# TensorE makes the level products of a head two at a time, at four places of its slabs instead of seven

## The chip, the cores and the metric

One core of one Trainium2 chip runs the whole program. The metric is the device time of that core in microseconds (us), the median of the runs. Every time below that is not a run's time is read from one profiled execution.

## The reference

One decoder layer over 1024 tokens of width 2048: an RMSNorm, one input projection whose columns feed two groups of heads (8 HGRN2 heads with a 128x128 state, 4 GLA heads with a 128x256 state), a gated linear recurrence per head, a per-head RMSNorm times SiLU(gate), the output projection, and a gated embedding on top. What the level products belong to is this part:

```python
b = jnp.cumsum(g_c, axis=2)                       # running sum of the log decay
diff = b[:, :, :, None, :] - b[:, :, None, :, :]
decay = jnp.where(causal, jnp.exp(jnp.where(causal, diff, 0.0)), 0.0)
attn = jnp.einsum('bhik,bhjk,bhijk->bhij', q_c, k_c, decay)
o = (jnp.einsum('bhij,bhjv->bhiv', attn, v_c)
     + jnp.einsum('bhik,bhkv->bhiv', q_c * jnp.exp(b), S))
```

## The kernel before

**Tiling.** The tokens are done in two halves of 512, `h` = 0 and 1. All large projections are made of slabs: a slab is 128 output columns times 2048 input rows, and TensorE makes it in 16 steps of `k`, each of three full-width matmuls (low weights with high activations, high with low, high with high; L505 to L507), so 48 matmuls of 512 columns into `acc[par]`. An HGRN head of the input projection takes 4 slabs, a GLA head 6.

**The recurrence rides on the slabs.** While TensorE makes the slabs of head `r0`, the recurrence of the head before it, `R = r0 - 1`, is done. Its TensorE work is hung on slab steps: `hooks[k]()` runs after the three matmuls of step `k`. With slabs of a head counted from 0, slab 0 has the transpose of the keys and the state update, slabs 1 and 2 have the seven level products, slab 3 the readout, and slab 3 or the one behind it the transposes of the output. The 24 heads of recurrence all go through `rec_hooks`: 14 during HGRN heads n = 1 to 7 of both halves, one during the first HGRN head of h = 1 (n = 0), eight during GLA heads (`gla_iteration`), and one, here called the last head, during the first slabs of the output projection (`last_head`). Where a position in a slab is named below, S1 and S2 are the starts of the first matmul of slab 1 and slab 2.

**The level products.** The causal attention inside a chunk of 128 tokens is built from LEVELS = 7 levels, l = 0 to 6, of block size 1, 2, 4, ... 64. For one level VectorE forms the exponents (`level_arg`, L1199 and L1200, into `x_lv[l % 3]`), ScalarE takes the exponential (`rec_level`, L801), VectorE multiplies keys and queries in (`level_mul`, L1206 and L1207, which raises `lv_in`), TensorE makes the product (`level`, L570, two instructions that the profile shows as four matmuls, into `lv_ps[l % 2]`, raising `lv_ready`), and VectorE copies what is valid into `attn` (`mask_level`: a small memset L1118 and a predicated copy L1214, which raises `masked`). VectorE goes on like this: the arguments of levels 0 to 2 and the multiplications of 0 and 1 come in `rec_first`; then `next_level(l)` is the mask of l, the multiplication of l + 2, the argument of l + 3. So the multiplication of level 5 stands behind the mask of level 3, and that of level 3 behind the mask of level 1.

**What stands between.** Each engine runs its queue in order. VectorE also makes the low part of the weights of each slab (`low_weights`, L1134, twice a slab), ScalarE the high part (`split_weights`, L737, twice a slab), which waits until the slab that used the buffer before is finished. In a GLA head ScalarE has `split_weights(s + 3, 1)` ahead of the exponential of level 5, in an HGRN head behind it:

```python
for l in (2, 3, 4):            # gla_iteration, ScalarE
    rec_level(R, l)
split_weights(s + 3, 1)
rec_level(R, 5)
```

In an HGRN head it is `for l in (2, 3)`, `for l in (4, 5)`, and then the split.

Of the kernel before, what the change touches and what calls it, by code (L numbers as in the profile page):

```python
# [141 lines left out]
def build(nc, x_feat, p, slabs, w_glr, w2, vec, lb_rows, masks, restart, ident_d, out, e_scratch, y_scratch):  # L142
    with ExitStack() as ctx:
# [359 lines left out]
        def _(pe):  # L503
# [36 lines left out]
            def k_transpose(R):  # L540
                pe.wait_ge(kt_ready, R + 1)
                pe.wait_ge(v_ready, R + 1)
                for c in range(NC_):
                    last = nc.tensor.transpose(tr_ps[:, c * P:(c + 1) * P], kt[:, c * C:(c + 1) * C], ident[:, :])  # L544
                last.then_inc(kttr_ready, 1)
                pe.wait_ge(qk_ready, R + 1)
                for c in range(NC_):
                    last = nc.tensor.matmul(ms_ps[:, c:c + 1], qk[:, c * C:(c + 1) * C], ones[:, 0:1],  # L548
                                            start=True, stop=True)
                last.then_inc(dgps_ready, 1)  # L550
# [4 lines left out]
            def state_update(R, nb):  # L555
                pe.wait_ge(ktpos_ready, R + 1)
                pe.wait_ge(o_copied, R + 1)
                for c in range(NC_):
                    last = nc.tensor.matmul(so_view(nb, c), kt_pos[:, c * P:(c + 1) * P],  # L559
                                            v_pos[:, c * nb * P:(c + 1) * nb * P], start=True, stop=True)  # L560
                last.then_inc(su_ready, 1)

            def level(R, l):
                pe.wait_ge(lv_in, R * LEVELS + (l + 1))
                pe.wait_ge(masked, R * LEVELS + (l + 1))
                half = C // 2
                for c in range(2):
                    queries = x_lv[l % 3][:, 2 * C:4 * C].rearrange("p (b n) -> p b n", b=2)
                    scores = lv_ps[l % 2][:, 0:2 * C].rearrange("p (b n) -> p b n", b=2)
                    last = nc.tensor.matmul(scores[:, :, c * half:(c + 1) * half], x_lv[l % 3][:, c * C:(c + 1) * C],  # L570
                                            queries[:, :, c * half:(c + 1) * half], start=True, stop=True)
                last.then_inc(lv_ready, 1)
# [27 lines left out]
                nc.tensor.matmul(ms_ps[:, :], w2_now[0:2 * RANK, :], glr_t[0:2 * RANK, :],  # L600
                                 start=True, stop=True).then_inc(logit_ready, 1)

            def levels(R, ls):
                return {k: (lambda l=l: level(R, l)) for k, l in ls}

            def glr_product(h):
                pe.wait_ge(glrw_ready, 1)
# [10 lines left out]

            def rec_hooks(R, nb):
                return [{7: lambda: k_transpose(R), 15: lambda: state_update(R, nb)},  # L620
                        levels(R, ((2, 0), (6, 1), (10, 2), (14, 3))),
                        levels(R, ((2, 4), (6, 5), (10, 6)))]

            def hgrn_iteration(h, n, rec_nb, first=False):

                r0 = h * HEADS + n
                R = r0 - 1
                hooks = [{}, {}, {}, {}]
                if rec_nb:
                    hooks = rec_hooks(R, rec_nb) + [{1: lambda: readout(R, rec_nb)}]  # L630
                    hooks[3][11] = lambda: o_transpose(R, rec_nb, glr_half=h if first else None)
                if first:
                    hooks[1][15] = lambda: glr_product(h)
                pair = t_of(s_in(h)) // 2
                hooks[3][15] = lambda: v_transpose(r0, 1, h, n * 2 + pair)
                for j in range(SLABS_H):
                    slab(n * SLABS_H + (s_in(h) + j), j % 2, n * 2 + (pair + j // 2), hooks[j],
                         fill=h if first and j == 0 else None)

            def gla_iteration(h, m, rec_nb, frees=False):  # L640
                r0 = h * HEADS + (m + NH)
                R = r0 - 1
                hooks = rec_hooks(R, rec_nb) + [
                    {1: lambda: gate_logits(r0, m), 7: lambda: readout(R, rec_nb)},
                    {13: lambda: o_transpose(R, rec_nb, m * 3 + (sp_no(h, 3 * NH) + 2))}, {}]
                pair = t_of(s_in(h) + NH * SLABS_H) // 2
                if h == 0 and rec_nb == 1:
                    hooks[4][8] = lambda: row_sums(ROWS_X[1], x_added, 2 * KT, sq_sum[:, :])
                hooks[5][11] = lambda: v_transpose(r0, 2, h, m * 3 + pair)
                for j in range(SLABS_G):  # L650
                    slab(m * SLABS_G + (s_in(h) + NH * SLABS_H + j), j % 2, m * 3 + (pair + j // 2), hooks[j],
                         frees=frees and j == SLABS_G - 1)
# [31 lines left out]

            R = HALVES * HEADS - 1
            last_head = rec_hooks(R, 2) + [{7: lambda: readout(R, 2)}, {13: lambda: o_transpose(R, 2)}, {}]

            def o_pair(h, i, hooks=({}, {}), fill=None, frees=False):
# [1051 lines left out]
```

## Time and profile before

| | us |
|---|---|
| median of 3 runs | 2266.56 |
| lowest, highest | 2266.39, 2266.7 |
| the profiled execution, its own time | 2266.82 |
| its span, first to last instruction | 2265.0 |

TensorE is busy for 98% of the span, VectorE 66%, ScalarE 44%. A matmul's record lasts until its end, and the next one starts before that, so the pace of TensorE is read from start to start, not from the durations.

### The profile page before, as it was taken

Reading aid. Unit: us, or ns where it says so; the run is one execution under the profiler, and the core shown is the slowest. Engines: PE = TensorE matmul, PEld = TensorE weight load, DVE = VectorE, ACT = ScalarE, POOL = GpSimd, SP = SyncE. Lnnn points to the kernel's source line nnn. Section 1 sums busy time; section 2 is a strip of 40 time slices with the busy share of each in tenths; the row PEclk is TensorE's granted clock in tenths of the full one; section 3 lists DMA queues with packets and bytes.
Section 4 is the critical chain, followed back from the end, with each engine's and each line's share of the span. In section 5 each row is a group of like instructions: output and inputs, shape, how many; then the busy total and the mean of one; then the engine's idle time right before and its main releaser. Section 6 shows DMA issues by size and latency. Waiting matters only on the chain.

```text
span 2265.0 us, 30797 instructions
## 1 busy us (share of the span) xinstructions
PE 2229.7 (98%) x10576; PEld 1858.2 (82%) x10576; DVE 1484.1 (66%) x2913; ACT 993.4 (44%) x1687; POOL 10.7 (0%) x12
## 2 busy tenths in 40 slices
PE   8999999999999999999999999999999999999995
PEld 7888888888888888888888888888888888887884
DVE  7567777775566666777776556566336448768876
ACT  6455544544333444444444333343224335546552
POOL 1000000000000000000000000000000000000000
PEclk9999999999999999999999999999999999999997
DMA  8522222222222224232222322222634553333442
GB/s 311 180 80 79 97 85 91 79 85 92 86 92 84 84 75 163 79 97 81 95 79 79 98 85 92 84 93 90 221 116 155 167 179 113 138 117 115 154 153 102
DMA packets 88502, 257.26 MB, mean 114 GB/s; under 512 B 9296, under 2 KB 9552, under 8 KB 88432
## 3 DMA queue, kind: packets, MB, share of 16 engines
q1 hardware_dynamic: 88432, 256.35, 33.6%
q8 instruction: 41, 0.67, 0.1%
q14 instruction: 29, 0.24, 0.0%
HBM read 231.15 MB, written 25.17 MB: 113 GB/s over the span
## 4 chain that ended last, share of the span: by engine, by line
PE 95%; DVE 2%; ACT 1%; DMA 1%; issue 0%; DVEq 0%; SPq 0%; ACTq 0%
PE acc L505 28%; PE acc L506 28%; PE acc L507 28%; PE lv L570 3%; PE so L581 1%; PE so L579 1%; PE so L559 1%; PE ms L548 1%; DMA w_raw<-in_slabs 1%; DVE sq_sum L1463 1%; DVE act_lo L1153 0%; PE tr L593 0%; PE tr L536 0%; PE tr L544 0%; DVE work L1635 0%
## 5 line engine op out<-in xcount | busy, mean ns | idle before, releaser
L505 PE MATMUL acc<-act_hi,w_lo 128*128 128x512 f32 x2880 | 1153.5, 401 | 1.5 <-DVE act_lo L1153 1.4
L506 PE MATMUL acc<-act_lo,w_hi 128*128 128x512 f32 x2880 | 1123.2, 390 | 0.0
L507 PE MATMUL acc<-act_hi,w_hi 128*128 128x512 f32 x2880 | 1123.0, 390 | 0.0
L505 PEld LDWEIGHTS acc<-act_hi,w_lo 128*128 128x128 f32 x2880 | 542.3, 188 | 114.3 <-issue 9.2
L507 PEld LDWEIGHTS acc<-act_hi,w_hi 128*128 128x128 f32 x2880 | 541.1, 188 | 114.3
L506 PEld LDWEIGHTS acc<-act_lo,w_hi 128*128 128x128 f32 x2880 | 542.4, 188 | 104.5 <-issue 2.0
L737 ACT CAST w_hi<-w_raw 128x1024 fp32r<-128x1024 f32 x356 | 358.0, 1047 | 508.0 <-PE acc L507 472.4
L1134 DVE TENSOR_TENSOR w_lo<-w_raw,w_hi 128x1024 fp32r<-128x1024 f32 x356 | 420.3, 1220 | 80.5 <-ACT w_hi L737 80.3
L801 ACT ACTIVATE work<-work 128x512 f32<-128x512 f32 x120 | 75.6, 630 | 169.9 <-DVE work L1200 169.2
L751 ACT ACTIVATE work<-work 128x512 f32<-128x512 f32 x96 | 60.7, 632 | 141.2 <-DVE work L1180 141.2
L1214 DVE COPY_PREDICATED work<-mask_sb,lv 128x256 f32<-128x256 uint8 x168 | 88.7, 528 | 7.3
L570 PEld LDWEIGHTS lv<-work 128*128 128x128 f32 x480 | 71.9, 190 | 9.3
L1206 DVE TENSOR_TENSOR work<-work 128x256 f32<-128x256 f32 x120 | 50.7, 423 | 38.5 <-ACT work L801 38.5
L570 PE MATMUL lv<-work 128*128 128x128 f32 x480 | 72.6, 273 | 0.0
L745 ACT ACTIVATE work<-work 128x512 f32<-128x512 f32 x104 | 65.8, 633 | 3.3
L747 ACT ACTIVATE work<-work 128x512 f32<-128x512 f32 x104 | 65.8, 633 | 3.3
L1012 ACT ACTIVATE work<-work 128x512 f32<-128x512 f32 x32 | 20.0, 624 | 93.9 <-DMA work<-e_scratch 91.3
L1118 DVE MEMSET vec_dummy<- 128x1 f32 x209 | 12.3, 59 | 71.1 <-PE lv L570 67.2
L1509 DVE TENSOR_TENSOR feat<-acc,state_h 128x512 f32<-128x512 f32 (+1 forms) x16 | 11.0, 686 | 69.4 <-PE acc L507 63.6
L1185 DVE SCALAR_TENSOR_TENSOR work<-acc,work 128x512 f32<-128x512 f32 x48 | 33.2, 692 | 33.8 <-ACT work L751 33.8
L1207 DVE TENSOR_TENSOR work<-work 128x256 f32<-128x256 f32 x120 | 50.2, 419 | 0.0
L1200 DVE TENSOR_TENSOR work<-work 128x256 f32<-128x256 f32 x120 | 50.1, 418 | 0.0
(215 smaller groups left out, 1777.8 us busy)
## 6 DMA issues: line engine op xcount, KB each, us to landing
w_raw<-in_slabs SPq DMA_DIRECT2D x356, 512.0 KB, 4.1
work<-e_scratch SPq DMA_DIRECT2D x64, 256.0 KB, 4.6
feat<-in_x_feat SPq DMA_DIRECT2D x8, 1024.0 KB, 12.4
e_scratch<-work SPq DMA_DIRECT2D x32, 256.0 KB, 4.5
state_h<-in_x_feat SPq DMA_DIRECT2D x32, 256.0 KB, 2.6
y_scratch<-work SPq DMA_DIRECT2D x16, 256.0 KB, 2.0
y_scratch<-work SPq DMA_DIRECT2D x8, 512.0 KB, 2.8
feat<-y_scratch SPq DMA_DIRECT2D x4, 1024.0 KB, 9.0
```

The source lines that it names most:

```text
L505: nc.tensor.matmul(ps, lhs_lo, rhs_hi, start=start, stop=False)
L506: nc.tensor.matmul(ps, lhs_hi, rhs_lo, start=False, stop=False)
L507: return nc.tensor.matmul(ps, lhs_hi, rhs_hi, start=False, stop=stop)
L570: last = nc.tensor.matmul(scores[:, :, c * half:(c + 1) * half], x_lv[l % 3][:, c * C:(c + 1) * C], queries[:, :, c * half:(c + 1) * half] ...
L737: nc.scalar.copy(w_hi[par][:, j, :], w_raw[j][:, :]).then_inc(w_hi_ready, 1)
L745: st.mark(A(t1, t1, ACT.Exp, scale=-1.0))
L747: A(t1, t1, ACT.Ln, bias=1.0).then_inc(sp_ready, 1)
L751: A(t2, t2, ACT.Exp).then_inc(sig_ready, 1)
L801: A(x_lv[l % 3], x_lv[l % 3], ACT.Exp).then_inc(lv_exp, 1)
L1134: v.tensor_tensor(w_lo[par][:, j, :], w_raw[j][:, :], w_hi[par][:, j, :].bitcast(F32), ALU.subtract).then_inc(w_lo_ready, 1)
L1206: st.mark(v.tensor_tensor(keys, keys, lower_tokens(k_t, s), ALU.mult))
L1214: v.copy_predicated(upper_tokens(attn, s), mask_sb[:, l, :].rearrange("p (b n s) -> p b n s", b=2, s=s), lv_ps[l % 2][:, 0:TH // 2].rearra ...
```

## The change

The seven products stand at four places. Levels 0 and 1 are made after step 5 of slab 1 (before: after steps 2 and 6), 2 and 3 after step 12 (before: 10 and 14), 4 and 5 after step 3 of slab 2 (before: 2 and 6), and 6 after step 10 as before. The instructions and their waits are the same; the other engines' programs are untouched.

```diff
-            def levels(R, ls):
-                return {k: (lambda l=l: level(R, l)) for k, l in ls}
+            def level_pair(R, l):
+                level(R, l)
+                level(R, l + 1)
...
             def rec_hooks(R, nb):
                 return [{7: lambda: k_transpose(R), 15: lambda: state_update(R, nb)},
-                        levels(R, ((2, 0), (6, 1), (10, 2), (14, 3))),
-                        levels(R, ((2, 4), (6, 5), (10, 6)))]
+                        {5: lambda: level_pair(R, 0), 12: lambda: level_pair(R, 2)},
+                        {3: lambda: level_pair(R, 4), 10: lambda: level(R, 6)}]
```

In slab 1 of a head, TensorE before has level 3 alone, after step 14, one step ahead of slab 2:

```order
L507 MATMUL acc<-act_hi,w_hi 128x512
L570 MATMUL lv<-work 128x2x64 [waits masked,lv_in]
L570 MATMUL lv<-work 128x2x64
L505 MATMUL acc<-act_hi,w_lo 128x512
L506 MATMUL acc<-act_lo,w_hi 128x512
L507 MATMUL acc<-act_hi,w_hi 128x512
L505 MATMUL acc<-act_hi,w_lo 128x512 [waits w_lo_ready,w_hi_ready,acc_free0]
```

The same place now, after step 12 of slab 1: level 3 stands right behind level 2.

```order
L507 MATMUL acc<-act_hi,w_hi 128x512
L570 MATMUL lv<-x_lv 128x2x64 [waits masked,lv_in]
L570 MATMUL lv<-x_lv 128x2x64
L570 MATMUL lv<-work 128x2x64 [waits masked,lv_in]
L570 MATMUL lv<-work 128x2x64
L505 MATMUL acc<-act_hi,w_lo 128x512
```

Level 3 moved ahead by two steps, level 2 back by two. In slab 2, TensorE before has level 5 after step 6, with twelve rows of L505 to L507 between it and level 4:

```order
L507 MATMUL acc<-act_hi,w_hi 128x512
L570 MATMUL lv<-x_lv 128x2x64 [waits masked,lv_in]
L570 MATMUL lv<-x_lv 128x2x64
L505 MATMUL acc<-act_hi,w_lo 128x512
L506 MATMUL acc<-act_lo,w_hi 128x512
```

And now, after step 3 of slab 2, behind level 4 (`lv<-work`):

```order
L507 MATMUL acc<-act_hi,w_hi 128x512
L570 MATMUL lv<-work 128x2x64 [waits masked,lv_in]
L570 MATMUL lv<-work 128x2x64
L570 MATMUL lv<-x_lv 128x2x64 [waits masked,lv_in]
L570 MATMUL lv<-x_lv 128x2x64
L505 MATMUL acc<-act_hi,w_lo 128x512
```

Level 5 moved ahead by three steps. ScalarE's order around the exponentials of levels 3 to 6 of a GLA head, the same before and now (L801 of `x_lv` is level 5, L737 the high weights for slab 3):

```order
L801 ACTIVATE work<-work 128x512 [waits lv_arg] x2
L737 CAST w_hi<-w_raw 128x1024 [waits raw_loaded0,acc_ready]
L737 CAST w_hi<-w_raw 128x1024 [waits raw_loaded1]
L801 ACTIVATE x_lv<-x_lv 128x512 [waits lv_arg]
L811 ACTIVATE work<-acc 128x512 [waits acc_ready]
L801 ACTIVATE work<-work 128x512 [waits lv_arg]
```

Nothing moved there; the wait for `acc_ready` in the second row is for the end of slab 1.

## Rows read from the trace of the kernel before

**Rows 1.** The page: shares, chain that ended last, and a costly group.

```profile
PE 2229.7 (98%) x10576; PEld 1858.2 (82%) x10576; DVE 1484.1 (66%) x2913; ACT 993.4 (44%) x1687; POOL 10.7 (0%) x12
...
PE 95%; DVE 2%; ACT 1%; DMA 1%; issue 0%; DVEq 0%; SPq 0%; ACTq 0%
...
L570 PE MATMUL lv<-work 128*128 128x128 f32 x480 | 72.6, 273 | 0.0
```

**Rows 2.** Timeline, TensorE, a GLA head: start us, duration us, instruction.

```profile
734.23 0.60 PE L570 MATMUL lv<-work 128*128 128x128 f32 x4
...
735.36 0.39 PE L505 MATMUL acc<-act_hi,w_lo 128*128 128x512 f32 x1
...
737.40 0.60 PE L570 MATMUL lv<-work 128*128 128x128 f32 x4
...
740.59 0.60 PE L570 MATMUL lv<-x_lv 128*128 128x128 f32 x4
```

**Rows 3.** Timeline, TensorE: larger groups of small matmuls between slab steps.

```profile
714.10 0.60 PE L544 MATMUL tr<-ident,work 128*128 128x128 f32 x4
714.54 0.95 PE L548 MATMUL ms<-ones,work 128*128 128x1 f32 x8
...
862.61 1.05 PE L559 MATMUL so<-work 128*128 128x128 f32 x8
```

**Rows 4.** Timeline, VectorE, the same GLA head: behind level 3, and level 5's multiplication.

```profile
734.90 0.06 DVE L1118 MEMSET vec_dummy<- 128x1 f32 x1 [1.32 <-PE lv L570]
...
738.12 0.43 DVE L1206 TENSOR_TENSOR x_lv<-x_lv,work 128x256 f32<-128x256 f32 x1 [2.69 <-ACT x_lv L801]
738.47 0.42 DVE L1207 TENSOR_TENSOR x_lv<-x_lv,work 128x256 f32<-128x256 f32 x1
```

**Rows 5.** Timeline, ScalarE, the same GLA head.

```profile
735.56 2.00 ACT L737 CAST w_hi<-w_raw 128x1024 fp32r<-128x1024 f32 x2 [3.58 <-PE acc L507]
737.47 0.63 ACT L801 ACTIVATE x_lv<-x_lv 128x512 f32<-128x512 f32 x1
```

**Rows 6.** Timeline, the GLA head before it: level 3, and level 5's multiplication.

```profile
656.07 0.60 PE L570 MATMUL lv<-work 128*128 128x128 f32 x4
...
660.39 0.42 DVE L1207 TENSOR_TENSOR x_lv<-x_lv,work 128x256 f32<-128x256 f32 x1
```

**Rows 7.** Timeline, TensorE, second HGRN head of h = 1: levels 0, 2, 3.

```profile
865.56 0.60 PE L570 MATMUL lv<-work 128*128 128x128 f32 x4
...
872.62 0.71 PE L570 MATMUL lv<-x_lv 128*128 128x128 f32 x4 [0.54 <-DVE x_lv L1207]
...
875.92 0.60 PE L570 MATMUL lv<-work 128*128 128x128 f32 x4
```

**Rows 8.** Timeline, VectorE, the same head, levels 0 to 3 and 5.

```profile
871.14 0.06 DVE L1118 MEMSET vec_dummy<- 128x1 f32 x1
...
871.78 0.45 DVE L1206 TENSOR_TENSOR x_lv<-x_lv,work 128x256 f32<-128x256 f32 x1
872.15 0.41 DVE L1207 TENSOR_TENSOR x_lv<-x_lv,work 128x256 f32<-128x256 f32 x1
...
874.27 0.42 DVE L1207 TENSOR_TENSOR work<-work 128x256 f32<-128x256 f32 x1
...
875.31 0.06 DVE L1118 MEMSET vec_dummy<- 128x1 f32 x1
...
877.44 0.06 DVE L1118 MEMSET vec_dummy<- 128x1 f32 x1
...
878.53 0.42 DVE L1207 TENSOR_TENSOR x_lv<-x_lv,work 128x256 f32<-128x256 f32 x1
```

**Rows 9.** Timeline, last head: level 0 on TensorE, multiplications of 2 and 3.

```profile
1539.48 0.60 PE L570 MATMUL lv<-work 128*128 128x128 f32 x4
...
1542.78 0.43 DVE L1206 TENSOR_TENSOR x_lv<-x_lv,work 128x256 f32<-128x256 f32 x1 [0.42 <-ACT x_lv L801]
...
1548.15 0.41 DVE L1207 TENSOR_TENSOR work<-work 128x256 f32<-128x256 f32 x1
```

## The prediction

> **What bounds the kernel now.** I read the page first. TensorE is busy for 98% of the span and carries 95% of the chain that ended last [rows 1], so the time is its queue: its instructions at their pace, plus every moment in which it waits. A change in its queue counts in full, and work of VectorE or ScalarE counts only where TensorE waits for it. Then I went through the timeline of TensorE, head by head, for all 24 recurrences, and beside each level product I put the end of the multiplication that feeds it.
>
> Pace first. In slab 2 of a GLA head, 9 slab matmuls lie between 735.36 and 737.40, so one takes 0.227 us from start to start and a step of three 0.68 us. From level 4 at 737.40 to level 5 at 740.59 are 3.19 us [rows 2] (3.18 in nearly all gaps): four steps are 2.72, so a level product that stands alone costs 0.463 us. Nothing waits there; the page's group of level products has 0.0 us of idle time before it [rows 1].
>
> Then the slack, which is the start of the product less the end of the second half of its multiplication (L1207). In 13 of the 14 HGRN heads n = 1 to 7 it is 2.5 us or more at every level. In a GLA head it is 740.59 - (738.47 + 0.42) = 1.70 us at level 5 [rows 2, 4]; four of the eight GLA heads have 1.70, four 1.61. The second HGRN head of h = 1 already waits at level 2: 0.54 us idle for VectorE [rows 7]. In the last head level 3 has 0.46 us: it starts at 1539.48 + 3 x 3.18 = 1549.02, and its multiplication ends at 1548.56 [rows 9].
>
> **The new places.** S1 is level 0's old start less 9 matmuls, 2.04 us. Old starts are S1 + 2.04, 5.22, 8.40 and 11.58 for levels 0 to 3, S2 + 2.04 and 5.22 for 4 and 5. A pair costs its inner step plus a product alone. The inner step isn't in the trace; the nearest row is the four key transposes followed by another group behind waits of its own, 714.54 - 714.10 = 0.44 us [rows 3]. So new starts are: level 0 at S1 + 6 x 0.68 = 4.08, level 1 at 4.52, level 2 at 13 x 0.68 + 0.90 = 9.74, level 3 at 10.18, level 4 at S2 + 2.72, level 5 at S2 + 3.16, level 6 within 0.05 us of its old place. Levels 1, 3 and 5 come 0.70, 1.40 and 2.06 us earlier, levels 0, 2 and 4 come 2.04, 1.34 and 0.68 later.
>
> **What pairing saves.** Two products alone cost 0.926. As a pair they cost 0.44 + 0.463 = 0.903, 0.023 less. The other bound is the state update, eight matmuls of 128 columns in one block: from 862.61 [rows 3] to level 0 at 865.56 [rows 7] are 2.95 us with 9 slab matmuls (2.04) in them, so the block costs 0.91, 0.016 less. I take 0.02: three pairs times 24 heads are 72, so 1.4 us less (bounds 1.2 and 1.7).
> On this the Trainium skill, page TensorE: Matmul & The Clock Gate, section Step-by-step: what each phase is for, says that the drain of one matmul overlaps the fill of the next, which gives no price to a border between two kinds of matmul at all. By that rule the 1.4 us are zero and the sum is that much higher. The block of eight agrees nearly.
>
> **What a wait costs.** One row shows it. Level 2 of the second HGRN head of h = 1 would start at 865.56 + 2 x 3.18 = 871.92. Its multiplication ends at 872.15 + 0.41 = 872.56 [rows 8], 0.64 late. The product starts at 872.62, 0.06 behind that, and level 3 follows 3.30 us later instead of 3.18 [rows 7], 0.12 more. So a product that is late by x costs x + 0.18.
> The same page, section LDWEIGHTS, gives a load of 128 columns as 128 / 1.2 = 107 ns, which is what is bare when a load can't run ahead of a wait; by that figure alone, estimated, ten waits would cost 0.7 us less than by the row.
>
> **Level 5 in GLA heads, eight times.** Its multiplication waits for ScalarE [rows 4], and ScalarE has two weight casts ahead of the exponential, which start when slab 1 ends: 735.56 to 737.5, exponential to 738.10, multiplication to 738.89 [rows 5, 4]. None of this depends on where levels 3 and 4 stand, as the argument of level 5 is done long before 737.47. So the multiplication still ends at S2 + 738.89 - 735.36 = S2 + 3.53, and the product now stands at S2 + 3.16: late by 0.37, cost 0.55 us. In the head before, S2 is 656.07 + 1.13 = 657.20 (1.13 from [rows 2]), the multiplication ends at 660.81 [rows 6], S2 + 3.61: late by 0.45, cost 0.63. Four of each: 4 x 0.55 + 4 x 0.63 = 4.7 us more. Queued behind level 5 on TensorE are only slab steps; what VectorE does next (low weights, then mask 4) doesn't wait for level 5, and level 6 has its input 0.7 us ahead before and more now, so there is no second wait.
>
> **Level 3 in the second HGRN head of h = 1.** Here VectorE is late from the start (late weights of slab 2), and its chain doesn't see the move: multiplication 3 ends at 874.27 + 0.42 = 874.69 [rows 8]. S1 is 863.52, level 3 now stands at 873.70: late by 0.99, cost 1.17, in place of the old wait at level 2 of 0.64 + 0.18 = 0.82. Net 0.35 us more.
>
> **Level 3 in the last head.** S1 is 1537.44, level 0 moves to 1541.52, and VectorE sees a product 0.67 us after its start (734.90 - 734.23) [rows 4, 2], so it masks from 1542.19. From that memset to the multiplication are 0.64 us (871.14 to 871.78) [rows 8], so 1542.83 instead of 1542.78 [rows 9]: 0.05 later, since it waited for ScalarE there before. Multiplication 3 ends at 1548.61, level 3 now stands at 1547.62: late by 0.99, cost 1.17 us.
>
> **Where the cover holds.** In the 13 other HGRN heads VectorE starts mask 0 at S1 + 4.08 + 0.67 = 4.75, up to 0.9 us later than now. From there to the end of multiplication 3 are 874.69 - 871.14 = 3.55 us [rows 8]: 8.30, level 3 at 10.18, 1.9 us to spare. Level 5: level 2 is seen at 9.74 + 0.67 = 10.41, the next mask is 877.44 - 875.31 = 2.13 later, the multiplication ends 878.95 - 877.44 = 1.51 behind it [rows 8]: 14.05, while level 5 stands at S1 + 15.86. In these heads the exponential of level 5 is ahead of the casts. Mask 4 and all behind it on VectorE (low weights of slab 3, the forget gate that frees `acc[1]`, masks 5 and 6) come 0.7 us later; slab 3 and the readout have over 1 us of room. Without this cover each 0.1 us would cost 1.3 us over 13 heads. The first HGRN head of h = 1 has less room at level 3, but `glr_product` stands ahead of its slab 2, so level 5 has more. No DMA moves but for those 0.7 us, and they land before the casts that wait for slabs.
>
> **The sum.** 4.7 + 0.35 + 1.17 - 1.4 = 4.8 us. The profiled execution took 2266.82 us (span 2265.0, 1.8 around it), so its like would take 2271.6; it stands 0.26 above the median of 2266.56, so I forecast a median of 2271.4 us. A measurement of this kernel can tell about 0.2%, 4.5 us, so 2271.1 is the border: the forecast lies just beyond it.
>
> **The rivals.**
> Borders dearer than I think, and so not slower at all. A level matmul's record lasts 0.273 us [rows 1], while four of them cost 0.463, 0.116 each: 0.16 us of overhang is hidden by the next one. Were it bare at each border, a merge would save 0.16, 72 merges 11.5 us, and the time would be 2266.6 + 6.2 - 11.5 = 2261.3, faster. It decides from (6.2 + 4.5) / 72 = 0.15 us a merge; from 0.023 on the result is within 0.2%. Against it: the block of eight costs 0.91, not 0.77 [rows 3]. Chance 0.05 for faster. A half-way price, some 0.05 us a merge (2269.2), 0.12, no change.
> Level 5 isn't late. Were the end of the multiplication seen earlier than its record ends, or the exponential earlier, the GLA heads would cost nothing: 2266.6 + 1.5 - 1.4 = 2266.7. For it: the lateness is only 0.4 us. Against it: the only wait in the trace ended 0.06 us behind the record. Chance 0.11.
> Waits dearer. Were the restart behind a wait that sits between two products as dear as a product alone (0.46 instead of 0.18), ten waits would cost 2.8 us more: 2274.2. Chance 0.12.
>
> **How the numbers follow.** The forecast's own case, 2270.4 to 2272.4, has 0.60; two thirds of it lie beyond 2271.1 (0.40), one third below (0.20). Slower 0.40 + 0.12 = 0.52, within 0.2% 0.20 + 0.12 + 0.11 = 0.43, faster 0.05. The range from 2268.8 to 2274.4 takes in the half-way price and the dear waits at 2274.2, and leaves out 2266.7 and 2261.3, 0.16, with what spills past either end under 0.2 in all.
>
> **What would show it.** In the profile after: level 5 of each GLA head with some 0.4 us of idle time before it, until VectorE's L1207, eight times; level 3 of the second HGRN head of h = 1 and of the last head with about 0.9; none in the ordinary HGRN heads. L1207 of level 5 still some 3.5 us behind the start of slab 2. The second product of a pair 0.44 us behind the first. Wrong would be: an inner step under 0.40 (pairing saves more), level 5 without a wait, or waits in HGRN heads.

## The result

The change makes the kernel slower by about what was forecast.

| | median us | lowest to highest | runs |
|---|---|---|---|
| before | 2266.57 | 2265.81 to 2267.26 | 15 |
| changed | 2271.4 | 2270.49 to 2272.05 | 15 |

The ratio is 1.0021, 95% interval 1.0013 to 1.0029: slower, and on the border of 0.2% that the prediction drew, not clearly beyond it. The difference of the medians is 4.8 us; the sum had 4.8. The spans of the two profiled executions, 2265.0 and 2269.7 us, differ by 4.7, at the same mean granted clock of 0.993 of full speed.

The waits of TensorE in the changed kernel, from the view that lists who waited for whom (waiting engine and tile, its line, what it waited for, us in all, times, longest). Lines behind the removed function are one higher than before, so VectorE's multiplication L1207 is L1208 here:

```profile
PE ms L618 <- DVE state_g L1628: 7.6, 1, 7.6
PE lv L618 <- DVE sq_sum L1464: 4.9, 1, 4.9
PE lv L570 <- DVE x_lv L1208: 2.3, 8, 0.3
PE lv L570 <- DVE work L1208: 1.8, 2, 0.9
PE tr L657 <- DVE ones L1449: 1.6, 1, 1.6
```

Before the change the same view had one wait at a level product, of 0.5 us. Now there are ten: eight at a product that reads `x_lv` (level 5) and two at one that reads `work` (level 3). The other waits are as before, but for two new ones of 0.3 and 0.2 us in the first 46 us, ahead of all level products. The chain that ended last, 95% on TensorE before, now goes over other engines where they are waited for:

```profile
PE 93%; DVE 3%; ACT 2%; DMA 1%; issue 1%; DVEq 0%; ACTq 0%; SPq 0%
```

**A GLA head.** The timeline of TensorE after, at the places of [rows 2]:

```profile
733.31 0.60 PE L570 MATMUL lv<-x_lv 128*128 128x128 f32 x4
733.76 0.61 PE L570 MATMUL lv<-work 128*128 128x128 f32 x4
...
738.98 0.60 PE L570 MATMUL lv<-work 128*128 128x128 f32 x4
739.84 0.71 PE L570 MATMUL lv<-x_lv 128*128 128x128 f32 x4 [0.25 <-DVE x_lv L1208]
...
745.18 0.60 PE L570 MATMUL lv<-work 128*128 128x128 f32 x4
```

The first pair, levels 2 and 3, runs through: the second product 0.45 us behind the first. In the second pair level 5 is 0.86 us behind level 4, not 0.44, and level 6 follows after 5.34 us where seven steps and one product alone (4.76 + 0.46) would be 5.22. So this head lost 0.42 + 0.12 = 0.54 us. The idle time that the view names, 0.25, is only part of it: it is counted from the modelled end of the product ahead. How much a head grows can be read without that, from one state update to the next. For the GLA head from 564 to 643 us, before and then after:

```profile
564.59 1.89 PE L559 MATMUL so<-work 128*128 128x256 f32 x8
...
642.75 1.89 PE L559 MATMUL so<-work 128*128 128x256 f32 x8
```

```profile
564.33 1.89 PE L559 MATMUL so<-work 128*128 128x256 f32 x8
...
643.07 1.89 PE L559 MATMUL so<-work 128*128 128x256 f32 x8
```

It took 78.16 us and takes 78.74. ScalarE and VectorE in the GLA head of [rows 2] again, the answer to [rows 5] and [rows 4]:

```profile
736.46 2.00 ACT L738 CAST w_hi<-w_raw 128x1024 fp32r<-128x1024 f32 x2 [3.27 <-PE acc L507]
738.36 0.63 ACT L802 ACTIVATE x_lv<-x_lv 128x512 f32<-128x512 f32 x1
```

```profile
739.02 0.43 DVE L1207 TENSOR_TENSOR x_lv<-x_lv,work 128x256 f32<-128x256 f32 x1 [2.69 <-ACT x_lv L802]
739.36 0.42 DVE L1208 TENSOR_TENSOR x_lv<-x_lv,work 128x256 f32<-128x256 f32 x1
```

Slab 2 starts at 738.98 - 2.72 = 736.26. The casts wait for the end of slab 1, the exponential for the casts, the multiplication for the exponential. It ends at 739.78, 3.52 us into slab 2 (forecast 3.53), and the product starts 0.06 us behind it, as in [rows 7, 8].

**The two heads that are late at level 3.** The second HGRN head of h = 1, TensorE:

```profile
868.91 1.05 PE L570 MATMUL lv<-work 128*128 128x128 f32 x8
...
874.58 0.60 PE L570 MATMUL lv<-x_lv 128*128 128x128 f32 x4
876.09 0.71 PE L570 MATMUL lv<-work 128*128 128x128 f32 x4 [0.90 <-DVE work L1208]
...
881.44 0.60 PE L570 MATMUL lv<-work 128*128 128x128 f32 x4
881.88 0.61 PE L570 MATMUL lv<-x_lv 128*128 128x128 f32 x4
```

Level 3 comes 1.51 us behind level 2 in place of 0.44, 1.07 late with the 0.06. With 0.12 behind it that is 1.19 us (forecast 1.17). The last head shows the same:

```profile
1550.77 0.60 PE L570 MATMUL lv<-x_lv 128*128 128x128 f32 x4
1552.25 0.71 PE L570 MATMUL lv<-work 128*128 128x128 f32 x4 [0.87 <-DVE work L1208]
```

1.48 us apart, so 1.04 + 0.12 = 1.16 (forecast 1.17). In the ordinary HGRN heads no product waits, as forecast. One of them, from state update to state update, before and then after:

```profile
436.69 1.05 PE L559 MATMUL so<-work 128*128 128x128 f32 x8
...
488.47 1.05 PE L559 MATMUL so<-work 128*128 128x128 f32 x8
```

```profile
435.98 1.05 PE L559 MATMUL so<-work 128*128 128x128 f32 x8
...
487.71 1.05 PE L559 MATMUL so<-work 128*128 128x128 f32 x8
```

That is 51.78 us before and 51.73 after. The shortest lead there of a multiplication's end over its product is 1.9 us, at level 3, as forecast.

### The profile page after: what moved, and what is told of

It reads as the page before. It is cut to its first block, busy times and chain, and to the rows that moved or that the text cites. A ratio compares the mean times of both kernels' runs of the same rounds, so it can differ in the third digit from the quotient of the medians.

```text
span 2269.7 us, 30797 instructions
## 1 busy us (share of the span) xinstructions
PE 2230.4 (98%) x10576; PEld 1858.0 (82%) x10576; DVE 1485.0 (65%) x2913; ACT 993.5 (44%) x1687; POOL 10.7 (0%) x12
## 4 chain that ended last, share of the span: by engine, by line
PE 93%; DVE 3%; ACT 2%; DMA 1%; issue 1%; DVEq 0%; ACTq 0%; SPq 0%
PE acc L505 28%; PE acc L506 27%; PE acc L507 27%; PE lv L570 3%; PE so L581 1%; PE so L579 1%; PE so L559 1%; ACT w_hi L738 1%; PE ms L548 1%; DMA w_raw<-in_slabs 1%; DVE sq_sum L1464 1%; DVE act_lo L1154 0%; PE tr L593 0%; PE tr L536 0%; PE tr L544 0%
## 5 line engine op out<-in xcount | busy, mean ns | idle before, releaser
L505 PE MATMUL acc<-act_hi,w_lo 128*128 128x512 f32 x2880 | 1147.1, 398 | 1.9 <-DVE act_lo L1154 1.4
L507 PE MATMUL acc<-act_hi,w_hi 128*128 128x512 f32 x2880 | 1122.6, 390 | 0.0
L505 PEld LDWEIGHTS acc<-act_hi,w_lo 128*128 128x128 f32 x2880 | 541.9, 188 | 117.9 <-issue 9.9
L507 PEld LDWEIGHTS acc<-act_hi,w_hi 128*128 128x128 f32 x2880 | 541.0, 188 | 114.1
L1207 DVE TENSOR_TENSOR work<-work 128x256 f32<-128x256 f32 x120 | 50.7, 422 | 37.6 <-ACT work L802 37.5
L570 PEld LDWEIGHTS lv<-work 128*128 128x128 f32 x480 | 66.5, 191 | 7.8 <-DVE work L1208 2.2
```

What stands on the lines that cost most here:

```text
L505: nc.tensor.matmul(ps, lhs_lo, rhs_hi, start=start, stop=False)
L507: return nc.tensor.matmul(ps, lhs_hi, rhs_hi, start=False, stop=stop)
L1207: st.mark(v.tensor_tensor(keys, keys, lower_tokens(k_t, s), ALU.mult))
```

## The experiments

They ran in two batches (1 to 4, and 5 to 8), each beside the kernel before, whose median was 2266.3 us in the first (27 runs) and 2266.43 in the second (33 runs), and 2266.57 in the result above. The changed kernel wasn't in these batches: "less" or "more than the change" is against the 2271.4 us of the result, and carries that shift of 0.1 to 0.3 us. Each edit is against the changed kernel. Three theories were set against each other: the waits of the prediction, a chain on VectorE that is shifted later in HGRN heads, and a border, a price of the pair itself (the expectations call the first two the wait theory and the delayed chain).

**1. Levels 4 and 5 one step later.**

```diff
-                        {3: lambda: level_pair(R, 4), 10: lambda: level(R, 6)}]
+                        {4: lambda: level_pair(R, 4), 10: lambda: level(R, 6)}]
```

> Levels 4 and 5 as a pair after step 4 of slab 2 instead of step 3; the rest as in the change. Wait theory (the loss is TensorE waiting for the multiplication of level 5 in eight GLA heads and of level 3 in two heads): level 5 stands at S2 + 3.84, its multiplication ends at S2 + 3.53 to 3.61, so the eight waits go and 4.7 us come back: 2266.7 us, two waits at level 3 left. Rival, delayed chain (the loss comes from VectorE's work that is shifted later in HGRN heads): level 4 moves later still, so no better than 2271.4. Rival, border (a pair itself costs more than two single places): unchanged, 2271.4.

Measured: 2267.22 us (2266.28 to 2267.7, 11 runs), ratio to before 1.0003 (0.9994 to 1.0012). Of the loss 4.2 us came back, though level 4 and VectorE's work behind it stand later still. TensorE's waits at level products:

```profile
PE lv L570 <- DVE work L1208: 2.0, 2, 1.1
```

The eight of `x_lv` are gone, the two of level 3 are left, one of them 0.2 us longer than in the change. That is some of the 0.5 us by which the time lies above the 2266.7 that was expected; the rest no trace shows.

**2. The exponential of level 5 ahead of the casts.** In `gla_iteration` on ScalarE:

```diff
-                split_weights(s + 3, 1)
                 rec_level(R, 5)
+                split_weights(s + 3, 1)
```

> The change as it is, and in GLA heads ScalarE takes the exponential of level 5 ahead of the two weight casts for slab 3 instead of behind them. Wait theory: the multiplication of level 5 ends before slab 2 begins or soon after, so TensorE doesn't wait at level 5: 4.7 us less than the change, 2266.7 us. If the multiplication is late for VectorE's own sake (its queue, not the exponential), it stays at 2271.4. Delayed chain and border: 2271.4.

Measured: 2266.7 us (2266.08 to 2267.26, 11 runs), ratio 1.0001 (0.9992 to 1.001), 4.7 us less than the change with TensorE's program untouched. ScalarE, VectorE and TensorE in the GLA head of above:

```profile
734.42 0.63 ACT L802 ACTIVATE x_lv<-x_lv 128x512 f32<-128x512 f32 x1 [2.69 <-DVE x_lv L1201]
735.01 2.01 ACT L738 CAST w_hi<-w_raw 128x1024 fp32r<-128x1024 f32 x2
```

```profile
735.09 0.43 DVE L1207 TENSOR_TENSOR x_lv<-x_lv,work 128x256 f32<-128x256 f32 x1 [0.19 <-ACT x_lv L802]
735.43 0.42 DVE L1208 TENSOR_TENSOR x_lv<-x_lv,work 128x256 f32<-128x256 f32 x1
```

```profile
737.53 0.60 PE L570 MATMUL lv<-work 128*128 128x128 f32 x4
737.97 0.61 PE L570 MATMUL lv<-x_lv 128*128 128x128 f32 x4
```

The multiplication ends at 735.85, over 2 us ahead of the product, and level 5 follows level 4 after 0.44 us. The casts lose nothing: they waited for slab 1 anyway. So the late input was ScalarE's order, not VectorE's queue.

**3. Only level 5 moved, no pairs.**

```diff
-                        {5: lambda: level_pair(R, 0), 12: lambda: level_pair(R, 2)},
-                        {3: lambda: level_pair(R, 4), 10: lambda: level(R, 6)}]
+                        {2: lambda: level(R, 0), 6: lambda: level(R, 1), 10: lambda: level(R, 2), 14: lambda: level(R, 3)},
+                        {2: lambda: level(R, 4), 3: lambda: level(R, 5), 10: lambda: level(R, 6)}]
```

> All seven products at places of their own, levels 0 to 4 where they were before the change, and only level 5 moved from step 6 to step 3 of slab 2. Wait theory: level 5 stands at S2 + 3.18, late by 0.35 to 0.43, eight times 0.53 to 0.61: 2266.6 + 4.6 = 2271.1 us, with the old wait at level 2 kept and none at level 3. Border: without pairs nothing is lost, 2266.6. Delayed chain: level 4 isn't moved, so 2266.6.

Measured: 2270.89 us (2269.99 to 2271.7, 11 runs), ratio 1.0021 (1.0012 to 1.003). One product moved by three steps, without any pairing, costs nearly as much as the whole change. Nine waits: the eight of level 5, and the old one of level 2.

```profile
PE lv L570 <- DVE x_lv L1208: 2.5, 9, 0.3
```

**4. Levels 4 and 5 one step earlier.**

```diff
-                        {3: lambda: level_pair(R, 4), 10: lambda: level(R, 6)}]
+                        {2: lambda: level_pair(R, 4), 10: lambda: level(R, 6)}]
```

> Levels 4 and 5 as a pair one step earlier still, after step 2 of slab 2; the rest as in the change. Wait theory: each of the eight waits grows by one step, 0.68 us: 5.4 us more than the change, 2276.8 us. Delayed chain: level 4 comes earlier, so 2271.4 or less. Border: the same number of pairs, 2271.4.

Measured: 2277.01 us (2276.34 to 2277.87, 5 runs), ratio 1.0046 (1.0032 to 1.006), 5.6 us more than the change. Its waits:

```profile
PE lv L570 <- DVE x_lv L1208: 7.8, 8, 1.0
```

7.8 in place of 2.3 us over eight heads is 0.69 each, one step. With experiment 1 this gives three points: a step later nothing, at the place of the change 0.6 us a head, a step earlier 1.3. What an input falls behind its product is paid in full.

**5. Levels 2 and 3 after step 14.**

```diff
-                        {5: lambda: level_pair(R, 0), 12: lambda: level_pair(R, 2)},
+                        {5: lambda: level_pair(R, 0), 14: lambda: level_pair(R, 2)},
```

> The change with levels 2 and 3 after step 14 instead of 12. Wait theory: the two waits at level 3 go (1.17 + 1.17 us), the eight at level 5 stay: 2271.4 - 2.3 = 2269.1 us. If levels 2 and 3 two steps later make VectorE late for level 5 in HGRN heads as well, there are up to 14 more waits: above 2271.4.

Measured: 2269.32 us (2268.34 to 2269.72, 11 runs), ratio 1.0012 (1.0003 to 1.0021), 2.1 us less than the change. Its trace has the eight waits of level 5 (2.3 us together) and none at level 3, and no wait at level 5 in HGRN heads either.

**6. Pairs where nothing is late.** Step 14 for levels 2 and 3 and step 4 for levels 4 and 5, the edits of 5 and 1 together.

> The same pairs at places where nothing is late: 0 and 1 after step 5 and 2 and 3 after step 14 of slab 1, 4 and 5 after step 4 of slab 2. Wait theory: level 3 stands at S1 + 11.54 as in the kernel before, so its two waits go, and the old wait at level 2 of the second HGRN head of h = 1 (0.82 us) goes too; level 5 isn't late. What is left is the price of 72 merges at 0.016 us (0.457 twice against 0.898, as the change's trace gives them): 2266.6 - 1.15 - 0.82 = 2264.6 us. Border (a pair is dearer than its parts): above 2266.6. Pairs worth something bigger: below 2263.

Measured: 2264.52 us (2263.84 to 2265.31, 11 runs), ratio 0.9992 (0.9983 to 1.0001). The trace has no wait at any level product; what is left is what the kernel before had elsewhere, but for the 0.3 us of the last line:

```profile
PE ms L618 <- DVE state_g L1628: 7.6, 1, 7.6
PE lv L618 <- DVE sq_sum L1464: 4.9, 1, 4.9
PE tr L657 <- DVE ones L1449: 1.6, 1, 1.6
PE acc L505 <- DVE act_lo L1154: 1.4, 2, 0.8
PE so L559 <- ACT work L806: 1.1, 1, 1.1
PE acc L505 <- issue: 0.3, 1, 0.3
```

The median is 1.9 us below that of before, as the sum of the merges and the lost wait at level 2 has it. The interval just takes in 1, so that it is faster is likely and not settled.

One lead has become very short in it. In the second HGRN head of h = 1, VectorE's multiplication of level 3 and TensorE's product:

```profile
873.39 0.42 DVE L1208 TENSOR_TENSOR work<-work 128x256 f32<-128x256 f32 x1
```

```profile
873.93 0.65 PE L570 MATMUL lv<-work 128*128 128x128 f32 x4
```

The input is there 0.12 us ahead of the product. The view names no wait, but the product's record is 0.65 us long in place of 0.60, and the head takes 51.79 us where the ordinary ones take 51.73.

**7. The same with the exponential first.** The edits of 6 and 2 together.

> As pairs_late, and the exponential of level 5 ahead of the casts in GLA heads. If the 0.2 to 0.3 us that pairs_late leaves between multiplication and product still cost something in the eight GLA heads, this is up to 1 us faster than pairs_late; by the wait theory it is the same, 2264.6 us.

Measured: 2264.61 us (2264.0 to 2264.84, 11 runs), ratio 0.9991 (0.9982 to 1.0): the same as 6. A lead of 0.24 to 0.32 us between the multiplication and its product, as the GLA heads have it in 6, is enough: they take 78.12 us in both. The 0.12 us of the HGRN head above were not quite; here that head has 0.38 us of lead and takes 51.73.

**8. The control: the same places, unpaired.** The edit of 2, and:

```diff
-                        {5: lambda: level_pair(R, 0), 12: lambda: level_pair(R, 2)},
-                        {3: lambda: level_pair(R, 4), 10: lambda: level(R, 6)}]
+                        {5: lambda: level(R, 0), 6: lambda: level(R, 1), 13: lambda: level(R, 2), 14: lambda: level(R, 3)},
+                        {3: lambda: level(R, 4), 4: lambda: level(R, 5), 10: lambda: level(R, 6)}]
```

> The control for pairs_late_exp5: the same order on ScalarE and the same latest place of each pair, but each product at a step of its own (0 to 3 after steps 5, 6, 13, 14 of slab 1, 4 and 5 after steps 3 and 4 of slab 2). No waits at any level, so what it takes beyond pairs_late_exp5 is what 72 merges are worth: 1.15 us by the costs of the places in the trace, so 2265.7 us; 0 if a border costs nothing; 3 us or more if it costs 0.05.

Measured: 2265.68 us (2264.84 to 2266.03, 11 runs), ratio 0.9997 (0.9988 to 1.0006), no wait at a level product. Beyond 7 it takes 1.07 us, 0.015 for each of 72 merges. The ranges of the two barely touch (2264.84 is the end of one and the start of the other).

## Why the prediction was right

The time, the way and the mechanism came out as forecast; point by point:

- **Level 5 in GLA heads**, 4.7 us forecast. The GLA head from 564 to 643 us took 78.16 us from state update to state update before and takes 78.74 now. With 0.05 for three merges added the wait there is 0.63, the forecast for that kind of head. The four of the other kind come out at 0.53 to 0.56 the same way (forecast 0.55). Experiments 1 and 2 take all eight waits away, by TensorE's place or by ScalarE's order alone, for 4.2 and 4.7 us; experiment 3 makes them without the rest of the change.
- **Level 3 in two heads**, 0.35 and 1.17 us forecast, 1.52 together. The waits measured 1.19 (less the old 0.82) and 1.16. Experiment 5 takes both away for 2.1 us; 2.34 was expected, which is the same within the scatter of the runs.
- **Pairing**, 1.4 us forecast from 0.02 a merge. The inner step of 0.44 us was right, and a pair now costs 0.90 us in the trace, two single places 0.91 to 0.92. Experiment 8 against 7 gives 1.07 us, 0.015 a merge. The value was a little high, because a product alone was put at 0.463 us and costs 0.46; the lower bound, 0.016 from the block of eight, was the nearer one. That a border is free altogether would have put experiment 8 at the time of 7.
- **The cover in HGRN heads** held. An ordinary HGRN head takes 51.73 us and took 51.78: faster by the three merges, with VectorE's masks later.
- **The rivals.** A border worth 0.05 us or more a merge would have put experiment 8 at 3.6 us above 7; it is excluded. That level 5 isn't late is excluded by its eight waits. That a wait inside a pair costs a whole product more is excluded by level 6 following after 5.34 us. The chain on VectorE, a rival of the experiments only, falls with 1 and 3.
- **What a wait costs**, x + 0.18 us for an input late by x, was read from one row and held at all ten waits: the product starts 0.05 to 0.06 us behind the end of the multiplication, and 0.11 to 0.15 us more are lost behind it (0.12 in the row).
- **The sum** hit 2271.4 to the tenth by luck. Its terms can be added up again in the two traces, from the first state update to level 6 of the last head, before and then after:

```profile
126.05 1.05 PE L559 MATMUL so<-work 128*128 128x128 f32 x8
...
1558.56 0.60 PE L570 MATMUL lv<-work 128*128 128x128 f32 x4
```

```profile
125.58 1.05 PE L559 MATMUL so<-work 128*128 128x128 f32 x8
...
1563.27 0.60 PE L570 MATMUL lv<-work 128*128 128x128 f32 x4
```

That stretch grew from 1432.51 to 1437.69 us, by 5.18: near the 6.2 us of waits, as forecast, less the 1.07 that experiment 8 gives for pairing, where 1.4 was forecast. So the sum of 4.8 was 0.3 to 0.4 too low. The profiled spans differ by only 4.7 because the recurrence of the changed kernel began 0.47 us earlier, in a part of the program that the change leaves alone; over the traces of all ten kernels that moment lies anywhere from 125.07 to 126.92 us. The medians, 4.8 apart, carry what is left of that scatter.

## What to carry to other kernels

When side work hangs on fixed steps of a queue that never idles, moving it earlier is free only down to the moment when its input is there: list, for every instance, the product's start less the end of the instruction that feeds it, and compare the move with the smallest, not the usual, value. Leave 0.2 us over: here 0.24 us of lead cost nothing and 0.12 cost 0.06. In the kernel before, HGRN heads had 2.5 us, GLA heads 1.6, and 2.06 were taken. Before giving an order up, look at what stands ahead of the late input on its own engine: two casts that would wait anyway sat in front of an exponential that was ready to go, and swapping them recovered the loss. Merging small groups of matmuls between large ones was worth 0.015 us a merge here, 1.07 us for all 72; each wait that it brought cost 0.5 to 1.2 us.

## What the runs showed that was not expected

The wait at level 3 in the second HGRN head of h = 1 isn't the same in each kernel: 0.90 us idle in the changed kernel, 1.1 in experiment 1, 0.47 in experiment 4, though the places of levels 2 and 3 are the same in all three. It follows the landing of the weights of slab 2, for which ScalarE waits there. Its first cast in the changed kernel, and in experiment 4:

```profile
869.02 1.05 ACT L738 CAST w_hi<-w_raw 128x1024 fp32r<-128x1024 f32 x1 [6.20 <-DMA w_raw<-in_slabs]
```

```profile
872.63 1.05 ACT L738 CAST w_hi<-w_raw 128x1024 fp32r<-128x1024 f32 x1 [5.74 <-DMA w_raw<-in_slabs]
```

The state update stands at 863.93 and 868.00 in the two, so the cast comes 5.09 and 4.63 us behind it, and the idle time differs by the same 0.4 us. So this one of the ten waits is half a matter of a transfer, and its size will vary from kernel to kernel. Why the landing moved stays open.

The weights of a late product are loaded late too. TensorE's weight loads for levels 4 and 5 in the GLA head of [rows 2], in the changed kernel:

```profile
738.76 0.64 PEld L570 LDWEIGHTS lv<-work 128*128 128x128 f32 x4
739.83 0.52 PEld L570 LDWEIGHTS lv<-x_lv 128*128 128x128 f32 x4 [0.44 <-DVE x_lv L1208]
```

Level 4's first load starts 0.22 us ahead of its product (738.98), level 5's together with its product (739.84), and the record of that product is 0.71 us long instead of 0.60. So 0.11 of the 0.12 us behind a wait is the time of a load that no longer runs ahead. It also fits the short lead in experiment 6: by x + 0.18 an input that is 0.12 us early would cost 0.06, which is what that head lost.

The idle time that the profile names before a late product understates the loss. At level 5 it reads 0.25 and 0.33 us, while the heads lost 0.54 and 0.63; the rest is the overlap of matmul records that a wait takes away and the 0.12 us behind it.
